# A chunked linear recurrence rewritten: 64-wide corner products, the inverse built apart from its right side, output and norm by token tile

## The chip, the cores and the metric

The kernel runs on one core of a Trainium2 chip. The metric is the device time of one execution in microseconds. Matrix products run on TensorE (PE), with weights loaded beside them (PEld); VectorE is DVE, ScalarE is ACT, GpSimd is POOL; SyncE (SP) issues DMAs. Each engine works through its own queue in order and waits on semaphores that other engines raise.

## What is computed

A model of two layers over 512 tokens of width 1024, and a third block of another kind. Each layer has feed-forward blocks, window attention, a gated memory (mlstm) and the recurrence that is changed here, with 4 heads of 64. For each head, token by token, the reference computes:

```python
def step(state, xs):
    r_t, w_t, k_t, v_t, a_t, b_t = xs
    sa = jnp.einsum('bhvk,bhk->bhv', state, a_t)
    state = (state * w_t[:, :, None, :] + sa[..., None] * b_t[:, :, None, :]
             + v_t[..., None] * k_t[:, :, None, :])
    return state, jnp.einsum('bhvk,bhk->bhv', state, r_t)
```

Ahead of it kk (the key times k_k, made unit length by head) gives a = -kk and b = kk times the rate. Behind it y is centred and normed by head, scaled by ln_w and ln_b, given the bonus sum(r k r_k) v, and multiplied by a gate.

## The kernel before

The stages of a layer run one after another, with a barrier of all engines between them: dense block, window attention, mlstm, `rwkv_stage` (L1340), dense block. In the dense blocks fp32 data are split in two parts and weights stream in by DMA. In `rwkv_stage` all data are in SBUF already, but for four small loads (L1395 to L1398).

Features lie on partitions, tokens on columns: 256 features are two tiles j of 128, with two heads each (halves q). The recurrence is done in chunks of 64 tokens. A token tile t of 128 holds two chunks, so its pair matrices are 128x128 with two blocks of 64x64 on the diagonal that count; masks put zeros elsewhere.

*Opening* (L1411 to L1434, L1564 to L1586, L1621 to L1661). The squares of kk are summed by head with a product by `halves` over 512 columns (L1413). DVE limits them (L1626), ACT takes roots (L1569), DVE takes reciprocals of 128x512 (L1631) and multiplies (L1632), `unit(0)` ahead of the two scans of L1638 and `unit(1)` behind them. Small products give decay, rate and gate (L1418 to L1425). ACT takes exponentials; DVE makes the factors f_a and f_b, POOL makes f_r and f_k (L1405, L1407).

*Tile loop* (L1487). `turn` transposes the factors of a tile to token rows, `pair` makes five pair matrices a head, DVE masks them (L1669), `a_values` (L1479) makes the right side X. Six steps follow. Each squares N and its transpose (L1498, L1502), which ACT (L1601) and DVE (L1687) copy out of PSUM, and adds N's power times X to X (L1507, L1691), X having 128 columns a head. Parts of the next tile's `prepare` stand between the steps. Then come the local products (L1517, L1523, L1524) and each chunk's step of state, G and H (L1531 to L1535).

*State loop* (L1539, L1705), behind all tiles: for 8 chunks PE makes G times state (L1543) and the state's share of y (L1549); DVE makes `carried` (L1709, L1711) and the next state (L1715).

*Norm* (L1552 to L1559, L1720 to L1737), over all 512 tokens with features on partitions: mean and variance with `halves`, root on ACT (L1615), reciprocal of 128x512 (L1732), and three more operations on DVE for each j.

Two pieces of code elsewhere matter for comparison: `mlstm_stage` has products of 128x128 by 65 columns (L1198), and `head_norm_stage` sums squares by token with two-column products (L1800).

## Time and profile before

| | us |
|---|---|
| median of 3 runs | 3401.26 (3397.11 to 3402.22) |
| profiled execution, its own time | 3395.85 |
| its span, first to last instruction | 3394.1 |
| PE busy | 3159.9 (93%) |
| DVE busy | 1449.1 (43%) |
| ACT busy | 1112.5 (33%) |
| mean granted TensorE clock | 0.947 of 2.4 GHz |

The span is the profiled execution between its first and last instruction; 1.75 us of the time lie around it. The clock is granted by a throttle in two levels, 1.2 and 2.4 GHz, and the page gives it as a share: 0.5 and 1.0. `rwkv_stage` runs from 686.3 to 848.1 us in the first layer and from about 2000 to 2165.1 in the second.

### The profile page before, as it was taken

Reading aid. Unit: us, or ns where it says so; the run is one execution under the profiler, and the core shown is the slowest. Engines: PE = TensorE matmul, PEld = TensorE weight load, DVE = VectorE, ACT = ScalarE, POOL = GpSimd, SP = SyncE. Lnnn points to the kernel's source line nnn. Section 1 sums busy time; section 2 is a strip of 40 time slices with the busy share of each in tenths; the row PEclk is TensorE's granted clock in tenths of the full one; section 3 lists DMA queues with packets and bytes.
Section 4 is the critical chain, followed back from the end, with each engine's and each line's share of the span. In section 5 each row is a group of like instructions: output and inputs, shape, how many; then the busy total and the mean of one; then the engine's idle time right before and its main releaser. Section 6 shows DMA issues by size and latency. Waiting matters only on the chain. (4 is left out here: it accounts for less than half of the span.)

```text
span 3394.1 us, 39653 instructions
## 1 busy us (share of the span) xinstructions
PE 3159.9 (93%) x16542; PEld 2654.7 (78%) x16542; DVE 1449.1 (43%) x1897; ACT 1112.5 (33%) x1566; POOL 174.1 (5%) x143
## 2 busy tenths in 40 slices
PE   8999997767999999999999769799999999999999
PEld 7888886556888878888887649588887877888887
DVE  3333414565433336233332564633325327555542
ACT  3222322331422236222222332322225335434431
POOL 0000005400000000000001620000000000000000
PEclk9999998688999999999999759899999989999999
DMA  3323221000223342223402000212234110122332
GB/s 131 100 93 112 94 75 41 1 12 1 100 81 99 110 139 75 75 94 112 136 32 90 1 11 1 94 40 97 99 106 144 50 57 25 44 72 91 97 97 83
DMA packets 71473, 255.64 MB, mean 75 GB/s; under 512 B 8056, under 2 KB 8952, under 8 KB 71296
## 3 DMA queue, kind: packets, MB, share of 16 engines
q1 hardware_dynamic: 71296, 253.12, 22.5%
q8 instruction: 131, 2.15, 0.3%
q14 instruction: 46, 0.38, 0.0%
HBM read 250.99 MB, written 2.10 MB: 75 GB/s over the span
## 5 line engine op out<-in xcount | busy, mean ns | idle before, releaser
L206 PE MATMUL ps<-h_hi,w_space 128*128 128x512 f32 (+3 forms) x5440 | 1504.8, 363 | 17.1 <-DVE h_lo L304 17.1
L206 PEld LDWEIGHTS ps<-h_hi,w_space 128*128 128x128 f32 x5440 | 982.0, 190 | 177.4 <-DVE h_lo L304 20.5
L194 DVE TENSOR_TENSOR w_space<-w_raw,w_space 128x1024 fp32r<-128x1024 f32 x440 | 536.2, 1225 | 1224.2 <-ACT w_space L187 1223.9
L206 PE MATMUL ps<-h_lo,w_space 128*128 128x512 f32 (+3 forms) x2720 | 986.1, 363 | 0.0
L187 ACT CAST w_space<-w_raw 128x1024 fp32r<-128x1024 f32 x440 | 457.9, 1047 | 1124.0 <-PE ps L206 726.0
L216 PE MATMUL ps<-w_space 128*128 128x512 f32 x3312 | 766.2, 393 | 35.0 <-DVE w_space L194 34.1
L216 PEld LDWEIGHTS ps<-w_space 128*128 128x128 f32 x3312 | 625.4, 190 | 166.9 <-issue 31.5
L206 PEld LDWEIGHTS ps<-h_lo,w_space 128*128 128x128 f32 x2720 | 516.5, 190 | 78.6
L579 ACT CAST w_space<-act_p 128x512 fp32r<-128x512 f32 x88 | 54.6, 621 | 187.4 <-DVE act_p L591 172.4
L594 DVE TENSOR_TENSOR w_space<-act_p,w_space 128x512 fp32r<-128x512 f32 x88 | 60.9, 693 | 69.9 <-ACT w_space L579 69.9
L591 DVE TENSOR_TENSOR act_p<-act_s,ps 128x512 f32<-128x512 f32 x88 | 59.9, 681 | 71.3 <-PE ps L206 71.3
L851 POOL MEMSET attn_v_tok<- 128x8 f32 x2 | 0.2, 114 | 1685.9 <-POOLq L86 1685.9
L264 ACT ACTIVATE junk<-x 128x1024 bf16<-128x1024 f32 x40 | 42.3, 1057 | 91.9 <-DVE x L285 80.5
L304 DVE TENSOR_TENSOR h_lo<-ps,h_hi 128x1024 fp32r<-128x1024 f32 x40 | 48.8, 1220 | 52.9 <-ACT h_hi L272 52.9
L216 PE MATMUL ps<-w_space,h_hi 128*128 128x512 f32 x256 | 69.2, 392 | 1.7 <-DVE h_lo L304 1.7
L575 ACT ACTIVATE act_s<-ps 128x512 f32<-128x512 f32 x88 | 52.2, 593 | 56.4 <-PE ps L206 56.4
L246 PE MATMUL ps<-mats,h_tokens 128*128 128x128 f32 x320 | 45.1, 287 | 22.5 <-DVE h_tokens L297 22.5
L628 ACT COPY proj<-ps 128x512 f32<-128x512 f32 x62 | 36.3, 585 | 83.5 <-PE ps L206 83.5
L1687 DVE COPY rwkv_power_t<-ps 128x512 f32<-128x512 f32 x40 | 27.7, 691 | 82.7 <-PE ps L1502 82.7
L2088 ACT ACTIVATE attn_probs<-ps 128x512 f32<-128x512 f32 x64 | 38.3, 599 | 71.3 <-PE ps L1998 71.0
L246 PEld LDWEIGHTS ps<-mats,h_tokens 128*128 128x128 f32 x320 | 38.9, 148 | 28.3 <-issue 13.9
L2008 PEld LDWEIGHTS ps<-v_tok,attn_probs 128*128 128x128 f32 x512 | 59.5, 192 | 1.3
(325 smaller groups left out, 2886.8 us busy)
## 6 DMA issues: line engine op xcount, KB each, us to landing
w_raw<-in_w_ffn_in SPq DMA_DIRECT2D x176, 512.0 KB, 3.5
w_raw<-in_w_ffn_out SPq DMA_DIRECT2D x88, 512.0 KB, 3.5
w_raw<-in_w_in SPq DMA_DIRECT2D x64, 512.0 KB, 3.6
w_raw<-in_w_up SPq DMA_DIRECT2D x44, 512.0 KB, 3.6
w_raw<-in_w_out SPq DMA_DIRECT2D x24, 512.0 KB, 3.6
w_raw<-in_w_down SPq DMA_DIRECT2D x22, 512.0 KB, 3.6
w_raw<-in_w_ple_gate SPq DMA_DIRECT2D x16, 512.0 KB, 5.0
gain_pre<-in_gains_pre SPq DMA_DIRECT2D x10, 512.0 KB, 4.6
```

What stands on the lines that cost most here:

```text
L187: nc.scalar.copy(self.hi(n), self.raw[:, n % SLOTS, :]).then_inc(self.hi_ready, 1)
L194: nc.vector.tensor_tensor(self.lo(n), self.raw[:, n % SLOTS, :], self.hi(n).bitcast(F32), ALU.subtract).then_inc(self.lo_ready, 1)
L206: m = nc.tensor.matmul(c.ps[:, bank, t], part[:, cols], moving[:, k, t], start=(k == 0 and i == 0), stop=(k == KD - 1 and i == 2))
L216: m = nc.tensor.matmul(c.ps[:, bank + half, :], x, part[:, half * S:(half + 1) * S], start=(first and i == 0), stop=(final and i == 2))
L246: m = nc.tensor.transpose(c.ps[:, self.bank(n) + k // 4, (k % 4) * P:(k % 4 + 1) * P], c.hn[:, k * P:(k + 1) * P], c.mat["ident"])
L264: nc.scalar.activation(c.junk[:, :], c.x[:, n, :], ACT.Square, accum_out=c.sums[:, 1, n:n + 1]).then_inc(c.pre_summed, 1)
L304: nc.vector.tensor_tensor(c.h_lo[:, :, t], pair(c, self.bank(n)).rearrange("p (k m) -> p k m", k=KD), c.h_hi[:, :, t].bitcast(F32), ALU.su ...
L575: nc.scalar.activation(c.s[:, q % 2, :], c.ps[:, self.bank(n), :], ACT.Silu).then_inc(c.silu_ready, 1)
L579: nc.scalar.copy(self.a.hi(q), c.p[:, q % 2, :]).then_inc(c.act_hi, 1)
L591: nc.vector.tensor_tensor(c.p[:, q % 2, :], c.s[:, q % 2, :], c.ps[:, self.bank(n), :], ALU.mult).then_inc(c.product, 1)
L594: nc.vector.tensor_tensor(self.a.lo(q), c.p[:, q % 2, :], self.a.hi(q).bitcast(F32), ALU.subtract).then_inc(c.act_ready, 1)
L2008: m = nc.tensor.matmul(c.ps[:, 5 + h % 2, at:at + DH + 1], probs[:, h % 2, j, n * P:(n + 1) * P], c.v_tok[:, j, v, :], start=(j == 0), sto ...
```

## The change

- In the opening the squares are summed by token: 16 products of 128 tokens by 2 columns. Floor, root and reciprocal then work on 128x16. ACT widens the result to 128x512 (`kk_wide`), PE transposes it back, and `unit` multiplies from PSUM; both units stand behind the scans.
- Pair matrices of a, and all that is built from them, are kept as 64x64 corners: chunk k on partition half k. A square is 16 products of 64x64 by 64, in one PSUM bank, copied by ACT alone.
- The inverse T is built by itself in five steps (identity + N, then T + power times T) of 64x64 by 64, and applied once to the right side (`solve`, 128 columns a head).
- State, output and norm of tile t-1 stand inside the loop of tile t. The output is made with tokens on partitions (`outputs`, 16 products of 128x128 by 64). The norm by token is a reduction over 64 columns a head; then two transposes (`turn_back`) and the last operations (`finish`).
- POOL zeroes `r_prime` once. The warm-up root on ACT (L1586) goes. The masks are a third of their size.

The order of PE's queue is in the diff; ACT's and DVE's follow it. DVE's order in tile t is: local and carry of t-1, inverse 1 and 2, next state, carry, inverse 3, next state, masks of a for t+1, centre, inverse 4, masks of r, corner values, variance, inverse 5, norm, finish. The diff is cut by 12 columns on the left; removed lines of the tile loop are those of the listing.

```diff
+    nc.gpsimd.memset(r_prime[:, :, :, :, :], 0.0).then_inc(padded, 1)
...
+    pe.wait_ge(kk_squared, 2)
     for j in range(2):
-        pe.wait_ge(kk_squared, j + 1)
-        nc.tensor.matmul(c.ps[:, 6 + j, :], c.mat["halves"], sq[:, j, :], start=True,
-                         stop=True).then_inc(kk_summed, 1)
+        for n in range(NT):
+            at = (j * NT + n) * 2
+            m = nc.tensor.matmul(c.ps[:, 6, at:at + 2], sq[:, j, n * P:(n + 1) * P],
+                                 c.mats[:, MATS.index("halves"), 0:P:DH], start=True, stop=True)
+    m.then_inc(kk_summed, 1)
...
+    for j in range(2):
+        pe.wait_ge(kk_widened, j + 1)
+        for n in range(NT):
+            m = nc.tensor.transpose(c.ps[:, 6 + j, n * P:(n + 1) * P], kk_wide[:, j, n, :, :], c.mat["ident"])
+        m.then_inc(kk_spread, 1)
     for j in range(2):
         pe.wait_ge(bonus_in, j + 1)
+        pe.wait_ge(lora_out, 4)
...
+    def corners(t, left, right, q, at):
+        for j in range(2):
+            for k in range(2):
+                cols, to = slice(t * P + k * CHUNK, t * P + (k + 1) * CHUNK), (2 * at + j) * CHUNK
+                m = nc.tensor.matmul(c.ps[half(k), ROW_BANKS[q], to:to + CHUNK], left[half(q), j, cols],
+                                     right[half(q), j, cols], start=True, stop=True)
+        return m
+    def pairs_of_a(t):
+        if t:
+            pe.wait_ge(gh_copied, 2 * (t - 1))
+        for q in range(2):
+            corners(t, f_a, f_b, q, N_LOW)
+            corners(t, f_b, f_a, q, N_UP)
+            m = corners(t, f_k, f_a, q, AK)
+        m.then_inc(pairs, 1)
...
+    def pairs_of_r(t):
+        pe.wait_ge(tok_ready, 2 * (t + 1))
         cols = slice(t * P, (t + 1) * P)
+        for o, left in ((RB, f_b), (RK, f_k)):
             for j in range(2):
+                for q in range(2):
+                    to = (2 * o + j) * P
+                    m = nc.tensor.matmul(c.ps[:, (AB_BANK, KV_BANK)[q], to:to + P], left[half(q), j, cols],
+                                         f_r[half(q), j, cols], start=True, stop=True)
+        m.then_inc(pairs, 1)
...
     def a_values(t):
+        pe.wait_ge(masked, 2 * t + 1)
+        for h, j, rows in heads:
+            for k in range(2):
+                m = nc.tensor.matmul(c.ps[half(k), ROW_BANKS[0], h * DH:(h + 1) * DH], pair_t[half(k), t % 2, AK, h, :],
+                                     tok[half(k), t % 3, QV, h * DH:(h + 1) * DH], start=True, stop=True)
         m.then_inc(av_done, 1)
...
+    def square(t, i):
+        n, n_t = parts(t, i - 1)
+        if i == 1:
+            pe.wait_ge(masked, 2 * t + 1)
+            if t:
+                pe.wait_ge(power_ready, STEPS * t)
+        else:
+            pe.wait_ge(power_ready, STEPS * t + i - 1)
+        for o, (a, b) in enumerate(((n_t, n), (n, n_t))):
+            if o == 0 or i < STEPS:
+                for h, j, rows in heads:
+                    for k in range(2):
+                        at = (o * R_HEADS + h) * CHUNK
+                        m = nc.tensor.matmul(c.ps[half(k), SQ_BANK, at:at + CHUNK], a[half(k), h, :],
+                                             b[half(k), h, :], start=True, stop=True)
+        m.then_inc(squared, 1)
+    def inverse(t, i):
+        pe.wait_ge(power_ready, STEPS * t + i)
+        if i == 1:
+            pe.wait_ge(t_first, t + 1)
+            if t:
+                pe.wait_ge(x_copied, t)
+        else:
+            pe.wait_ge(t_ready, STEPS * t + i - 1)
+        for h, j, rows in heads:
+            for k in range(2):
+                m = nc.tensor.matmul(c.ps[half(k), T_BANK, h * CHUNK:(h + 1) * CHUNK], parts(t, i)[0][half(k), h, :],
+                                     T[half(k), t % 2, h, :], start=True, stop=True)
+        m.then_inc(t_done, 1)
+    def solve(t):
+        pe.wait_ge(t_ready, STEPS * (t + 1))
+        pe.wait_ge(av_copied, t + 1)
+        for h, j, rows in heads:
+            for k in range(2):
+                m = nc.tensor.matmul(c.ps[half(k), T_BANK, h * P:(h + 1) * P], T[half(k), t % 2, h, :],
+                                     tok[half(k), t % 3, QA:QX + 1, h * DH:(h + 1) * DH], start=True, stop=True)
+        m.then_inc(x_done, 1)
+    def local(t):
+        pe.wait_ge(x_copied, t + 1)
+        pe.wait_ge(masked, 2 * (t + 1))
+        if t:
+            pe.wait_ge(state_ready, 2 * t + 1)
+        for h, j, rows in heads:
+            m = nc.tensor.matmul(c.ps[rows, S_BANK, j * P:(j + 1) * P], X[:, t % 2, h, 0, :], r_t[:, t % 2, RB, h, :],
+                                 start=True, stop=True)
+        m.then_inc(r_done, 1)
+    def steps_of_state(t):
+        pe.wait_ge(av_copied, min(t + 2, NT))
+        for k in range(2):
+            for h, j, rows in heads:
+                hc, at = slice(h * DH, (h + 1) * DH), j * P
+                nc.tensor.matmul(c.ps[rows, ROW_BANKS[k], at:at + DH], X[half(k), t % 2, h, 0, :],
+                                 tok[half(k), t % 3, QB, hc], start=True, stop=True)
+                o = c.ps[rows, ROW_BANKS[k], at + DH:at + P]
+                nc.tensor.matmul(o, tok[half(k), t % 3, QB, hc], X[half(k), t % 2, h, 1, :], start=True, stop=False)
+                m = nc.tensor.matmul(o, tok[half(k), t % 3, QK, hc], tok[half(k), t % 3, QV, hc], start=False,
+                                     stop=True)
+            m.then_inc(gh_done, 1)
+    def next_state(n):
+        t = n // 2
+        pe.wait_ge(gh_copied, n + 1)
+        pe.wait_ge(r_ready, t + 1)
+        pe.wait_ge(state_ready, n + 1)
+        for h, j, rows in heads:
+            at = 2 * P + j * DH
+            m = nc.tensor.matmul(c.ps[rows, S_BANK, at:at + DH], GH[rows, t % 2, n % 2, j, 0:DH],
+                                 state[rows, n, j, :], start=True, stop=True)
+        m.then_inc(state_done, 1)
+    def outputs(t):
+        pe.wait_ge(r_ready, t + 1)
+        pe.wait_ge(state_ready, 2 * t + 2)
+        if t:
+            pe.wait_ge(out_ready, t)
+        for h, j, rows in heads:
+            o = c.ps[:, Y_BANK, h * DH:(h + 1) * DH]
+            nc.tensor.matmul(o, r_t[:, t % 2, RB, h, :], X[:, t % 2, h, 1, :], start=True, stop=False)
+            nc.tensor.matmul(o, r_t[:, t % 2, RK, h, :], tok[:, t % 3, QV, h * DH:(h + 1) * DH], start=False, stop=False)
+            for k in range(2):
+                m = nc.tensor.matmul(o, r_prime[:, j, h % 2, k, :], state[:, 2 * t + k, j, :], start=False, stop=(k == 1))
+        m.then_inc(y_done, 1)
+    def turn_back(t):
+        pe.wait_ge(normed, t + 1)
+        for j in range(2):
+            m = nc.tensor.transpose(c.ps[:, Y_BANK, (2 + j) * P:(3 + j) * P], y[:, 2 * j:2 * j + 2, :],
+                                    c.mat["ident"])
+        m.then_inc(turned_back, 1)
...
     for t in range(NT):
+        more = t + 1 < NT
+        square(t, 1)
+        if t:
+            local(t - 1)
+            steps_of_state(t - 1)
+        square(t, 2)
+        inverse(t, 1)
+        if more:
+            turn(t + 1)
+        square(t, 3)
+        inverse(t, 2)
+        if t:
+            next_state(2 * t - 2)
+        square(t, 4)
+        inverse(t, 3)
+        if t:
+            outputs(t - 1)
+            next_state(2 * t - 1)
+        if more:
+            pairs_of_a(t + 1)
+        square(t, 5)
+        inverse(t, 4)
+        if more:
+            pairs_of_r(t + 1)
+        inverse(t, 5)
+        if more:
             a_values(t + 1)
+        if t:
+            turn_back(t - 1)
+        solve(t)
+    local(NT - 1)
+    steps_of_state(NT - 1)
+    next_state(NCH - 2)
+    outputs(NT - 1)
+    turn_back(NT - 1)
...
-        act.wait_ge(kk_floor, j + 1)
-        nc.scalar.activation(kk_len[:, j, :], kk_len[:, j, :], ACT.Sqrt).then_inc(kk_root, 1)
+    act.wait_ge(kk_floor, 1)
+    nc.scalar.activation(kk_len[:, :, :, :], kk_len[:, :, :, :], ACT.Sqrt).then_inc(kk_root, 1)
     nc.scalar.activation(lora[:, 1, :], mix[:, G_T, :], ACT.Sigmoid).then_inc(lora_in, 1)
     for j in range(2):
-        act.wait_ge(lora_done, j + 1)
...
+        powers(t, 1)
+        if t:
+            steps_of_state(t - 1)
+        powers(t, 2)
+        if t + 1 < NT:
+            rows_of(t + 1)
+        for i in range(3, STEPS + 1):
+            powers(t, i)
+        if t:
+            squares(t - 1)
+            root(t - 1)
+        solution(t)
+    steps_of_state(NT - 1)
+    squares(NT - 1)
+    root(NT - 1)
...
-    for j in range(2):
-        dve.wait_ge(kk_summed, j + 1)
-        nc.vector.tensor_scalar(kk_len[:, j, :], c.ps[:, 6 + j, :], 1e-24, None, ALU.max).then_inc(kk_floor, 1)
+    dve.wait_ge(kk_summed, 1)
+    nc.vector.tensor_scalar(kk_len[:, :, :, :].rearrange("p j n q -> p (j n q)"), c.ps[:, 6, 0:4 * NT], 1e-24,
+                            None, ALU.max).then_inc(kk_floor, 1)
+    dve.wait_ge(kk_root, 1)
+    nc.vector.reciprocal(kk_len[:, :, :, :], kk_len[:, :, :, :]).then_inc(kk_inverted, 1)
 
     def unit(j):
-        dve.wait_ge(kk_root, j + 1)
+        dve.wait_ge(kk_spread, j + 1)
         dve.wait_ge(kk_raw, 2)
-        ch.link(nc.vector.reciprocal(kk_len[:, j, :], kk_len[:, j, :]))
-        ch.link(nc.vector.tensor_tensor(kk[:, j, :], kk[:, j, :], kk_len[:, j, :], ALU.mult))
...
+    def centre(t):
+        dve.wait_ge(y_done, t + 1)
+        if t:
+            dve.wait_ge(turned_back, t)
+        o = by_head(quarter(Y_BANK, 0))
+        nc.vector.tensor_reduce(y_mean[:, :], o, AX, ALU.add).then_inc(y_summed, 1)
+        dve.wait_ge(y_summed, t + 1)
+        nc.vector.scalar_tensor_tensor(out=y[:, :, :], in0=y_mean[:, :].unsqueeze(2).to_broadcast([P, R_HEADS, DH]),
+                                       scalar=-1.0 / DH, in1=o, op0=ALU.mult, op1=ALU.add).then_inc(centred, 1)
+    def variance(t):
+        dve.wait_ge(y_squared, t + 1)
+        nc.vector.tensor_reduce(y_var[:, :], y_sq[:, :, :], AX, ALU.add).then_inc(var_summed, 1)
+    def norm(t):
+        dve.wait_ge(var_root, t + 1)
+        nc.vector.reciprocal(y_inv[:, :], y_var[:, :]).then_inc(var_inverted, 1)
+        dve.wait_ge(var_inverted, t + 1)
+        nc.vector.tensor_tensor(y[:, :, :], y[:, :, :], y_inv[:, :].unsqueeze(2).to_broadcast([P, R_HEADS, DH]),
+                                ALU.mult).then_inc(normed, 1)
+    def finish(t):
+        cols = slice(t * P, (t + 1) * P)
+        dve.wait_ge(turned_back, t + 1)
+        for j in range(2):
+            ch.link(nc.vector.tensor_scalar(out[:, j, :], c.ps[:, Y_BANK, (2 + j) * P:(3 + j) * P], vcol("ln_w", j),
+                                            vcol("ln_b", j), ALU.mult, ALU.add))
+        ch.link(nc.vector.tensor_tensor(out[:, :, :], out[:, :, :], bonus[:, :, cols], ALU.add))
+        nc.vector.tensor_tensor(c.y[:, 6:8, cols], out[:, :, :], gate[:, :, cols], ALU.mult).then_inc(out_ready, 1)
+    ch.wait()
+    dve.sem_inc(state_ready, 1)
+    dve.wait_ge(padded, 1)
```

## Rows read from the trace of the kernel before

**Rows 1.** Busy time by stretch of core 0, with granted clock (PEclk).

```profile
core 0: us, PE busy (x) PEld busy (x) DVE busy (x) ACT busy (x) POOL busy (x), PEclk, DMA share, GB/s
640.00:682.00 42.00, 35.16 (x108) 24.43 (x107) 25.46 (x67) 9.62 (x21) 15.94 (x16) 0.50 0.00 1
686.30:715.60 29.30, 11.68 (x20) 3.56 (x20) 24.57 (x26) 16.89 (x24) 6.36 (x4) 0.67 0.10 32
715.60:724.65 9.05, 6.56 (x56) 5.76 (x56) 5.02 (x13) 1.48 (x3) 0.00 (x0) 0.81 0.01 2
748.88:773.10 24.22, 23.34 (x259) 22.08 (x257) 11.75 (x23) 5.43 (x11) 0.00 (x0) 1.00 0.01 1
818.80:821.50 2.70, 1.36 (x32) 1.12 (x32) 2.34 (x10) 0.00 (x0) 0.00 (x0) 1.00 0.03 6
821.50:830.00 8.50, 6.72 (x96) 5.59 (x96) 7.13 (x31) 0.00 (x0) 0.00 (x0) 0.50 0.00 0
830.00:848.10 18.10, 6.19 (x8) 1.97 (x8) 13.76 (x12) 2.56 (x4) 0.00 (x0) 0.69 0.00 0
2029.10:2165.10 136.00, 112.80 (x1160) 101.19 (x1160) 71.47 (x146) 24.45 (x48) 0.00 (x0) 0.88 0.00 1
```

**Rows 2.** Timeline of PE, tile from 748.88: start, us, line, shapes, count.

```profile
747.17 0.32 PE L1531 MATMUL ps<-rwkv_tok,rwkv_x 64*64 64x64 f32 x2
...
749.87 1.06 PE L1502 MATMUL ps<-rwkv_n_t,rwkv_n 128*128 128x128 f32 x8
...
755.30 1.26 PE L1457 MATMUL ps<-proj 64*128 64x128 f32 x16
...
769.88 0.66 PE L1517 MATMUL ps<-rwkv_rb_t,rwkv_x 128*64 128x128 f32 x8
```

**Rows 3.** Timeline of PE and DVE in the state loop.

```profile
818.93 0.45 PE L1543 MATMUL ps<-rwkv_state,rwkv_gh 64*64 64x64 f32 x8 [0.64 <-DVEq L1704]
...
819.65 0.47 DVE L1715 SCALAR_TENSOR_TENSOR rwkv_state<-ps,rwkv_decay,rwkv_carried 128x64 f32<-128x64 f32 x2
...
821.64 0.69 PE L1543 MATMUL ps<-rwkv_state,rwkv_gh 64*64 64x64 f32 x8 [0.72 <-DVEq L1719]
```

**Rows 4.** Durations of single records by line: ns min/median/max.

```profile
L1543 PE MATMUL ps<-rwkv_state,rwkv_gh x128: 218/311/366, 818.9 to 2145.6; 64*64 64x64 f32 x128
...
L1444 PE MATMUL ps<-mats,proj x64: 272/273/447, 715.7 to 2093.2; 128*128 128x128 f32 x64
...
L1198 PE MATMUL ps<-mlstm_v_tok,mlstm_weighted x160: 417/417/477, 645.9 to 1993.1; 128*128 128x65 f32 x160
```

**Rows 5.** Timeline of PE at the lower clock.

```profile
675.12 4.53 PE L1198 MATMUL ps<-mlstm_v_tok,mlstm_weighted 128*128 128x65 f32 x20 [1.81 <-DVE mlstm_weighted L1311]
...
715.66 1.94 PE L1444 MATMUL ps<-mats,proj 128*128 128x128 f32 x8 [2.21 <-DVE proj L1657]
```

**Rows 6.** Timeline of ACT, DVE and POOL in the opening.

```profile
687.85 1.15 ACT L1565 ACTIVATE rwkv_sq<-rwkv_kk 128x512 f32<-128x512 f32 x2 [5.68 <-DVE rwkv_kk L1622]
...
700.15 0.69 DVE L1641 TENSOR_TENSOR proj<-rwkv_cum,rwkv_sig_w 128x512 f32<-128x512 f32 x1
...
706.95 1.65 POOL L1407 TENSOR_TENSOR proj<-rwkv_sig_w,rwkv_grow 128x512 f32<-128x512 f32 x1 [4.97 <-DVE rwkv_sq L1650]
...
707.50 1.37 DVE L1646 TENSOR_SCALAR rwkv_sig_w<-rwkv_rate,vecs 128x512 f32<-128x512 f32 x1
```

**Rows 7.** The head norm's sum by token: timeline, and durations by line.

```profile
2775.84 1.84 PE L1800 MATMUL ps<-mats,headnorm_sq 128*128 128x2 f32 x8 [0.44 <-ACT headnorm_sq L1846]
...
L1800 PE MATMUL ps<-mats,headnorm_sq x104: 167/251/354, 2767.6 to 2794.8; 128*128 128x2 f32 x104
```

**Rows 8.** Timeline of DVE in the norm.

```profile
836.74 3.35 DVE L1732 RECIPROCAL rwkv_cum<-rwkv_cum 128x512 f32<-128x512 f32 x1 [1.41 <-ACT rwkv_cum L1615]
```

**Rows 9.** Timeline of ACT and DVE in the tile from 748.88.

```profile
753.62 0.59 ACT L1601 COPY rwkv_power<-ps 128x512 f32<-128x512 f32 x1 [2.97 <-PE ps L1498]
...
769.98 0.42 DVE L1675 COPY rwkv_x<-ps 128x256 f32<-128x256 f32 x1
```

416 lines of the change are left out of this document (186 added, 230 removed).

## The prediction

> **What bounds the kernel now.** I read the page first: PE is busy 93% of the span and the chain that ended last is dense products, so a stage is worth what its own last wait is worth. The change touches only the recurrence, which runs once in each of two layers, so I cut the trace there. The table by stretch [rows 1] shows the first run: an opening on DVE and ACT of 29.3 us, 9.05 us of first pairs, three token tiles of 24.2 us from 724.65 on and a last one that is left with 21.5, a state loop of 11.2 (818.80 to 830.00) and a norm of 18.1. From the first transpose (715.66) to the last DVE instruction (848.08) that is 132.4 us; the second run takes 136.0 (2029.16 to 2165.1). Barriers stand at both ends, so what the stage loses or gains the kernel does.
>
> In a tile PE is busy 23.3 of 24.2 us: it is the bound there. In the state loop and the norm it is not; there DVE and PE hand one small thing back and forth [rows 3], and the norm has two reciprocals of 3.35 us [rows 8].
>
> The last thing to see is the clock. It stands at 1.00 (2.4 GHz) through the tiles, whose products are 128x128, and in 818.80 to 821.50. Then, with nothing in the queue but 64x64 products, it is at 0.50 (1.2 GHz), although PE is busy 6.7 of 8.5 us. The stretch 640 to 682 of the stage before has PE busy 84% and the clock at 0.50 throughout [rows 1]. So on this kernel a busy queue does not by itself hold the upper level.
>
> **PE's price for each shape.** A merged row less its last product, over the products before it, gives the step (two records make one fp32 product, one a transpose). At the upper level: 128x128 on 128 columns, (1.06 - 0.27)/7 = 0.112 us a record, the transposes of L1444 alike; 64 rows with 128 columns, (1.26 - 0.27)/15 = 0.066; 128x128 on 64 columns is taken like the full one, 0.11 (its weights are as wide); 128x64 on 128 columns, (0.66 - 0.27)/7 = 0.055; the 48 records of 64x64 from 747.17 to the next tile at 748.88, 0.036 [rows 2]; 64x64 on the two diagonal quarters in turn, (0.45 - 0.22)/7 = 0.033 [rows 3, 4]. At the lower: the same quarters (0.69 - 0.31)/7 = 0.054 [rows 3]; a transpose (1.94 - 0.45)/7 = 0.213; 128x128 on 65 columns (4.53 - 0.42)/19 = 0.216 [rows 5]. The shapes with no row at the lower level lie between their upper price and twice it; since 0.112 becomes 0.213 and 0.11 becomes 0.216, I take near twice: 0.107 where two tiles overlap, 0.057 for the 0.036. The new product of the solution, 64x64 on 128 columns, has no row: at least 0.033, at most 0.112; I take 0.055, its nearest, and 0.107.
>
> **The loop over tiles.** A tile in the middle, by records. Quarters: squares 4x32 + 16, inverse 5x16, corner values 16, two states 16, together 256 (once 128 of the full ones). Pairs of a and the state's steps: 96 at the 0.036 price. Transposes forth and back: 10. Outputs by token, four products a head with 128-column weights: 32. Pairs of r: 16. Local 8 and solution 16: 24.
> - Upper: 256x0.033 + 96x0.036 + 10x0.112 + 32x0.11 + 16x0.066 + 24x0.055 = 8.4 + 3.5 + 1.1 + 3.5 + 1.1 + 1.3 = 18.9 us.
> - Lower: 13.8 + 5.5 + 2.1 + 6.9 + 1.7 + 2.6 = 32.6 us.
>
> To these come handovers. Tile 748.88 sums by the same prices to 128x0.112 + 40x0.066 + 8x0.112 + 8x0.11 + 24x0.055 + 48x0.036 = 21.8 of its 24.2 us, so 2.4 us of switching and waiting. After, one wait is plain: the back transpose asks for the norm, and variance stands on DVE behind the corner copy, then root on ACT, reciprocal and product on DVE (0.42 + 0.42 + 0.3 + 0.2 + 0.42 with hops of 0.04 to 0.14), and the solution stands behind it on PE: 2.2 us. With 1.2 for switches that is 3.4 at the lower level (36.0 us a tile) and, with a wait for the last inverse step, 4.2 at the upper (23.1). DVE has about 12 us and ACT about 6 in a tile (a copy of 512 columns on ACT 0.59, one of 256 on DVE 0.42 [rows 9]): neither is the bound. That squares are copied by ACT alone costs 0.1 in copy, and is hidden while PE works on the inverse.
>
> The first tile lacks state, outputs and back transpose: 240x0.054 + 48x0.057 + 8x0.213 + 16x0.107x2 = 20.8 and 3.2 of waits = 24.0 (upper 15.9). The last lacks transposes, pairs and corner values (7.0): 29.0 (18.4). The opening pairs: 7.2 (4.8).
>
> **The end.** State loop and norm over 512 columns go (29.3 us). In their place stands, after the last solution: copy and local 2.0, state's steps 2.7, the carry and next state 2.4 (0.47 on DVE for the state itself [rows 3], as much for the carry, the rest hops), outputs 7.0, centre, square, variance, root, reciprocal, product 3.3, back transpose and four last operations 2.0: about 18.7 with 0.7 less of outputs and steps hidden; at the upper level 13.2.
>
> Lower level: 7.2 + 24.0 + 36.0 + 36.0 + 29.0 + 18.7 = 150.9, against 132.4 and 136.0: +18.5 and +14.9. Upper: 4.8 + 15.9 + 23.1 + 23.1 + 18.4 + 13.2 = 98.5: -33.9 and -37.5.
>
> **The opening on DVE.** Two reciprocals of 512 columns (6.7 us) leave DVE's path. In comes a sum by token: 16 products of two columns with 128-column weights, 32 records. The head norm's row gives (1.84 - 0.25)/7 = 0.23 us a record [rows 7]; at the transposes' 0.213, which lies next to it, they take 6.8 us, from the end of ACT's squares at 689.0 [rows 6] to 696.0. Square root, a table load, ACT's sigmoid and two copies of 0.6 follow, and the lora products stand behind the 32 records on PE, so ACT gives the first decay input at 700.1 and both scans and differences end at 703.9; before, the last of them, L1641, ended at 700.8 [rows 6]. The reciprocal that stood behind it is gone, but a second unit product (0.69) and POOL's first operation come in: a DVE instruction waits out POOL's (L1646 took 1.37 beside POOL's 1.65 [rows 6], twice what its plain form takes). I get +0.7 us a layer; bounds -2.5 (records at 0.112) to +2.5 (all four POOL operations in the way). POOL's memset of r_prime is unpriced, between 0.2 and 3.3 (two POOL operations), and has 25 us before anyone asks. The mask load shrinks behind other loads: nothing. A square-root table load moves to the second tile, 1.3 at most, beside DVE's variance.
>
> **Which level.** Full-array products give way to quarters with waits between them; the only such stretch in the trace lost the upper level. I take the lower, with one short upper stretch a layer (transposes and pairs raised it at 715.60 [rows 1]), worth 1.5 each. Sum: 18.5 + 14.9 + 1.4 - 3.0 = +32 us on the profiled 3395.85; that run is 5.4 under the median of those shown, 3401.26. The prediction is 3433.
>
> The Trainium skill, "TensorE: Matmul & The Clock Gate", Part 1, says the lower level is the default and that activity lifts it; by that rule read as busy time, this loop, busy nine tenths, would keep 2.4 GHz and the sum would be the upper one. The row of 640 to 682, 84% busy at 0.50, speaks against reading it so.
>
> **Rivals.**
> - *The loop keeps the upper level, but for a few falls* (PE leaves the bound mostly; this ends on the other side). For it: PE never idles over 2.2 us in a tile, and 64-row pairs in the opening ran with the clock up. Against: 821.50 to 830.00. It decides once the granted clock of the middle tiles reads above 0.9. -33.9 - 37.5 + 1.4 = -70 if it never falls, with cold openings and a fall in each tile -60: 3341. The point where it turns: a middle tile under about 30 us.
> - *Half and half*: outputs, transposes and pairs of r lift the level once a tile and quarters drop it. Between the sums, middle tiles of 29 to 30 us: +8, 3409.
> - *The change doesn't shorten the end*, because outputs by token (32 records a tile at 0.216) only trade the norm for PE time: that is inside the first sum; without the end's saving of 10.6 us a layer the time would be 3454. For it speaks only the wait for the norm.
>
> **Chances.** Lower level 0.51, half and half 0.16, upper 0.30, long end 0.03. Within 0.2% (about 7 us) of 3401 is what a measurement here can't tell from no change. Of the half case 0.06 lies below, 0.04 within, 0.06 above; of the lower case 0.02 below. Faster 0.38, same 0.04, slower 0.58. The likeliest case alone reaches from 3415 to 3446 (PE steps 6% off, opening bounds). The range takes in the upper case: 3332 to 3446.
>
> **What would show it.** The clock in the tile loop: 0.5 to 0.6 bears me out, 0.9 the rival. L1543's successors and the squares at 0.054 a record. A middle tile of 36 us against 23. The end at 19 us after the last solution. The opening at 30 us, with the sum by token at 6.8. Wrong would be: quarters that hold the clock at 1.00, or steps of quarters under 0.05 at the lower level.

## The result, and the profile after

The changed kernel takes 3317.73 us (median of 4 runs, 3314.60 to 3323.63) against 3400.45 us before (4 runs, 3397.11 to 3402.22). The ratio is 0.976, with a 95% interval of 0.9743 to 0.9777: 83 us faster. The forecast was 3433, with a range down to 3332; the result lies outside it on the fast side, past even the rival at 3341. The profiled execution took 3315.65 us, its span is 3313.8, and its mean granted clock 0.950.

Granted clock and busy time by stretch, changed kernel, first run of the stage (opening, first pairs, four tiles, end), then three stretches of 3.4 us (two around the end of the second tile, one in the last tile), then opening and rest of the second run:

```profile
core 0: us, PE busy (x) PEld busy (x) DVE busy (x) ACT busy (x) POOL busy (x), PEclk, DMA share, GB/s
685.90:711.60 25.70, 14.55 (x40) 7.59 (x40) 16.84 (x23) 15.38 (x23) 6.92 (x5) 0.63 0.09 26
711.60:718.80 7.20, 7.16 (x88) 6.51 (x90) 3.50 (x7) 1.07 (x2) 0.00 (x0) 0.50 0.01 2
718.80:733.70 14.90, 13.07 (x336) 12.17 (x334) 5.84 (x13) 3.79 (x7) 0.00 (x0) 0.93 0.01 3
733.70:755.50 21.80, 19.19 (x440) 17.92 (x437) 11.10 (x33) 7.12 (x13) 0.00 (x0) 0.99 0.01 2
755.50:778.40 22.90, 20.29 (x438) 18.82 (x436) 11.62 (x34) 5.83 (x12) 0.00 (x0) 0.94 0.01 3
778.40:796.00 17.60, 15.36 (x350) 14.08 (x344) 9.02 (x30) 4.83 (x11) 0.00 (x0) 1.00 0.01 3
796.00:809.20 13.20, 7.04 (x98) 6.22 (x98) 6.53 (x20) 1.98 (x5) 0.00 (x0) 0.89 0.01 1
751.60:755.00 3.40, 1.55 (x32) 1.25 (x29) 2.63 (x8) 0.95 (x2) 0.00 (x0) 1.00 0.00 0
755.00:758.40 3.40, 3.40 (x49) 2.95 (x45) 1.15 (x3) 1.17 (x2) 0.00 (x0) 0.51 0.02 5
792.00:795.40 3.40, 1.65 (x29) 1.38 (x31) 2.35 (x8) 0.71 (x2) 0.00 (x0) 1.00 0.00 0
1961.60:1987.20 25.60, 14.10 (x41) 7.34 (x41) 16.81 (x24) 15.38 (x23) 6.91 (x5) 0.63 0.09 26
1987.20:2083.60 96.40, 80.71 (x1728) 74.49 (x1728) 47.51 (x133) 24.63 (x49) 0.00 (x0) 0.92 0.01 2
```

These answer to [rows 1]. The tiles hold 0.93 to 1.00. The level comes up at 720.9, 2 us into the first tile; from there on no stretch of the tiles is at 0.50 but 3.4 us from 755.0, behind a stretch in which PE was busy 1.55 of 3.4 us. In the second run it is again one stretch of 3.4 us (2028.2). Against the stretches of before: opening 28.3 to 25.7 us in both layers; first transpose to last DVE operation 132.4 to 97.5 and 136.0 to 96.3. Together that is 5.3 + 34.9 + 39.7 = 79.9 of the 80.3 us by which the span got shorter. The rest of the kernel together moved by 0.4 us.

PE in the changed kernel, by timeline:

```profile
718.82 1.92 PE L1512 MATMUL ps<-rwkv_pair_t 64*64 64x64 f32 x32
721.43 1.15 PE L1512 MATMUL ps<-rwkv_power 64*64 64x64 f32 x32 [0.69 <-ACT rwkv_power L1676]
...
732.75 1.09 PE L1536 MATMUL ps<-rwkv_tok,rwkv_inverse_t 64*64 64x128 f32 x16 [0.92 <-DVE rwkv_inverse_t L1807]
...
753.97 0.44 PE L1590 MATMUL ps<-mats,rwkv_y 128*128 128x128 f32 x2 [1.84 <-DVE rwkv_y L1864]
...
806.67 0.69 PE L1590 MATMUL ps<-mats,rwkv_y 128*128 128x128 f32 x2 [2.88 <-DVE rwkv_y L1864]
```

A square of 32 records takes 1.92 us at 0.50 and 1.15 at 1.00: (1.92 - 0.31)/31 = 0.052 and (1.15 - 0.22)/31 = 0.030 a record, where the sum had 0.054 and 0.033 [rows 3, 4]. The solution, (1.09 - 0.27)/15 = 0.055 a record, is as assumed.

The opening, ACT and DVE beside PE, which answers to [rows 6] and [rows 7]:

```profile
687.61 3.57 PE L1417 MATMUL ps<-mats,rwkv_sq 128*128 128x2 f32 x16 [3.84 <-ACT rwkv_sq L1641]
...
691.68 0.25 DVE L1728 RECIPROCAL rwkv_kk_len<-rwkv_kk_len 128x16 f32<-128x16 f32 x1 [0.28 <-ACT rwkv_kk_len L1644]
...
694.97 1.27 ACT L1651 ACTIVATE rwkv_sig_w<-ps,vecs 128x512 f32<-128x512 f32 x2 [0.36 <-PE ps L1426]
695.76 1.23 DVE L1738 TENSOR_TENSOR_SCAN rwkv_cum<-rwkv_reset,rwkv_sig_w 128x512 f32<-128x512 f32 x1 [3.83 <-ACT rwkv_sig_w L1651]
```

The sum by token is 16 records, where the prediction had 32. The code issues eight products for it (two tiles of features times four of tokens), not 16 as was said of the change; at two records a product, as everywhere, that is 16.

### The profile page after: what moved, and what is told of

The parts are those of the page before. It is cut to its first block and busy times, and to the rows that moved or that the text cites. A ratio compares the mean times of both kernels' runs of the same rounds, so it can differ in the third digit from the quotient of the medians.

```text
span 3313.8 us, 42013 instructions
## 1 busy us (share of the span) xinstructions
PE 3106.2 (94%) x17718; PEld 2614.0 (79%) x17718; DVE 1385.5 (42%) x1867; ACT 1109.9 (33%) x1566; POOL 175.5 (5%) x145
## 5 line engine op out<-in xcount | busy, mean ns | idle before, releaser
L206 PEld LDWEIGHTS ps<-h_hi,w_space 128*128 128x128 f32 x5440 | 981.7, 190 | 177.8 <-DVE h_lo L304 20.3
L216 PE MATMUL ps<-w_space 128*128 128x512 f32 x3312 | 767.9, 393 | 15.9 <-DVE w_space L194 15.0
L2266 ACT ACTIVATE attn_probs<-ps 128x512 f32<-128x512 f32 x64 | 38.3, 599 | 71.4 <-PE ps L2176 71.1
L272 ACT CAST h_hi<-ps 128x1024 fp32r<-128x1024 f32 x40 | 40.3, 1007 | 57.6 <-PE ps L246 57.6
```

The lines of the kernel that those rows point to most:

```text
L206: m = nc.tensor.matmul(c.ps[:, bank, t], part[:, cols], moving[:, k, t], start=(k == 0 and i == 0), stop=(k == KD - 1 and i == 2))
L216: m = nc.tensor.matmul(c.ps[:, bank + half, :], x, part[:, half * S:(half + 1) * S], start=(first and i == 0), stop=(final and i == 2))
```

## The experiments

Two questions: what holds or drops the clock in this stage, and what each part of the change is worth. "Theory A" is one and the same in all of them: PE's waits between products let the clock fall, whatever the products' shape. "Fillers" are products or transposes whose result nobody reads, put where PE would wait. The same kernel's median moves by some us between chips, so each run's ratio is to runs of the kernel before on its own chip (0.976 for the changed kernel), and profiles are compared by the length of the stage, first to last DVE operation: 160.7 and 164.3 us before, 123.3 and 122.0 after. Medians that differ by 3 to 7 us can have overlapping intervals; where they do, the text says so.

| run | median us | ratio (95%) | stage, layer 1 / 2 |
|---|---|---|---|
| state_filled (of before) | 3397.43 | 0.9997 (0.9986 to 1.0009) | 163.1 / 163.2 |
| new_opening (of before) | 3392.77 | 0.9981 (0.9970 to 0.9993) | 157.6 / 158.2 |
| copy_six | 3397.26 | 0.9998 (0.9983 to 1.0012) | 166.5 / 160.3 |
| squares_twice | 3354.47 | 0.9866 (0.9851 to 0.9880) | 140.7 / 138.9 |
| norm_behind | 3335.62 | 0.9810 (0.9787 to 0.9832) | 129.8 / 127.4 |
| state_behind | 3364.52 | 0.9895 (0.9872 to 0.9918) | 150.8 / 145.4 |
| behind_filled | 3352.59 | 0.9850 (0.9821 to 0.9879) | 137.4 / 137.1 |
| back_late | 3320.85 | 0.9765 (0.9751 to 0.9780) | 123.5 / 123.1 |
| back_mid | 3324.13 | 0.9780 (0.9761 to 0.9798) | 125.7 / 126.2 |
| opening_filled | 3316.56 | 0.9751 (0.9731 to 0.9771) | 119.5 / 120.4 |
| end_filled | 3319.66 | 0.9766 (0.9747 to 0.9786) | 125.5 / 122.0 |
| all_filled | 3308.07 | 0.9728 (0.9707 to 0.9749) | 117.5 / 117.3 |
| lora_first | 3306.71 | 0.9730 (0.9708 to 0.9752) | 116.8 / 118.0 |
| outputs_split | 3301.45 | 0.9707 (0.9686 to 0.9729) | 115.0 / 116.3 |

### Fillers in the old state loop (state_filled)

```diff
                         m.then_inc(y_state, 1)
+                    for i in range(8):
+                        rows = slice(DH * (i % 2), DH * (i % 2) + DH)
+                        nc.tensor.matmul(c.ps[rows, 5, 0:DH], c.mat["ident"][rows, 0:DH], c.mat["halves"][rows, 0:DH],
+                                         start=True, stop=True)
```

> The kernel before, with eight products of 64x64 on the two quarters (16 records) added behind each of the eight steps of the state loop, into a bank that nobody reads, where PE waits 0.64 to 0.72 us for DVE in each step. Theory A (waits between the products let the clock fall, whatever their shape): the granted clock stays at 1.00 through the state loop, where it read 0.50 from 821.5 to 830.0, and the loop of 11.2 us gets 1 to 1.5 us shorter a layer, 3396 to 3400 in all. Theory B (as the prediction took it: a queue of nothing but 64x64 products doesn't hold the upper level): 0.50 as before, the fillers take 16 x 0.054 = 0.9 us a step at that level and overhang the wait by 0.2, so the loop gets 1 to 2 us longer a layer, 3403 or more.

Its state loop ran from 823.5 to 834.7. By stretch:

```profile
814.70:818.10 3.40, 1.68 (x15) 1.33 (x14) 1.81 (x3) 0.00 (x0) 0.00 (x0) 1.00 0.00 0
818.00:821.50 3.50, 3.42 (x33) 3.09 (x35) 0.45 (x2) 0.37 (x1) 0.00 (x0) 0.51 0.00 0
821.50:834.70 13.20, 10.62 (x301) 9.41 (x297) 9.47 (x40) 0.75 (x2) 0.00 (x0) 1.00 0.01 2
```

On DVE, the seventh of eight equal steps and the start of the eighth:

```profile
831.92 0.29 DVE L1713 TENSOR_TENSOR rwkv_carried<-rwkv_state,rwkv_gh 128x128 f32<-128x128 f32 x1
832.24 0.42 DVE L1715 TENSOR_SCALAR rwkv_carried<-rwkv_carried,rwkv_decay 128x64 f32<-128x64 f32 x2
832.70 0.47 DVE L1719 SCALAR_TENSOR_TENSOR rwkv_state<-ps,rwkv_decay,rwkv_carried 128x64 f32<-128x64 f32 x2
833.32 0.29 DVE L1713 TENSOR_TENSOR rwkv_carried<-rwkv_state,rwkv_gh 128x128 f32<-128x128 f32 x1
```

The loop holds nothing but 64x64 products, and the clock read 1.00 throughout, where it fell to 0.50 before. That bears out theory A on the clock: the waits drop it, the shape doesn't. Its time was wrong: the loop still takes 11.2 us, a step 1.40, because DVE's chain (carried, carried, state) sets the step at either level. Here, where PE isn't the bound, the level that came back gave nothing. The stages are 2.4 us longer and 1.1 shorter than before's; outside the loop the clock fell at other places (818.1 here, 821.5 there), and the median is the same. The first two rows are worth a look too: in the second, PE is busy 3.42 of 3.50 us with the clock at 0.51, and in the 3.4 us ahead of it PE had been busy only 1.68. The level of a stretch answers to what PE did before it.

### Waits put into the new tiles (copy_six)

```diff
                     else:
+                        for dst in (cum[:, 0, :], cum[:, 1, :], rate[:, 0, :], rate[:, 1, :], sig_w[:, 0, :]):
+                            nc.scalar.copy(dst, c.ps[:, SQ_BANK, :])
                         nc.scalar.copy(power[:, i % 2].rearrange("p o h n -> p (o h n)"), c.ps[:, SQ_BANK, :]).then_inc(power_ready, 1)
```

> The changed kernel, with ACT copying each of the first four squares six times (five extra copies of 0.59 us into tiles that are free by then). PE's instructions are unchanged; only waits come in. A square is 1.1 us of PE, then 3.5 of ACT, so a middle tile would be some 5 x 4.9 + 5 = 28 to 30 us if PE kept the upper level, with PE busy about 19 of them. Theory A (waits let the clock fall): the granted clock reads 0.50 in a good part of the tiles, the middle tile is over 31 us, the kernel 3375 or more. Theory B' (the mix of shapes sets the level, and this mix holds it): the clock stays at 1.00 but for what it falls now, the middle tile is 27 to 29, the kernel 3345 to 3370.

Its two middle tiles of the first layer, which run the same instructions, and PE's waits in the second of them:

```profile
744.90:772.80 27.90, 20.36 (x440) 18.72 (x438) 11.69 (x34) 16.62 (x33) 0.00 (x0) 0.95 0.01 2
772.80:806.50 33.70, 26.80 (x436) 25.04 (x434) 11.74 (x35) 15.34 (x32) 0.00 (x0) 0.75 0.01 2
```

```profile
777.36 1.15 PE L1512 MATMUL ps<-rwkv_power 64*64 64x64 f32 x32 [0.85 <-ACT rwkv_power L1678]
...
781.64 1.15 PE L1512 MATMUL ps<-rwkv_power 64*64 64x64 f32 x32 [1.64 <-ACT rwkv_power L1678]
...
785.92 1.15 PE L1512 MATMUL ps<-rwkv_power 64*64 64x64 f32 x32 [2.43 <-ACT rwkv_power L1678]
```

With waits of 0.85, 1.64 and 2.43 us ahead of the squares the clock falls again and again (mean of the span 0.934 against 0.950), and the change's whole gain is gone. Not all of these 80 us are the clock's: the waits by themselves were put at 3345 to 3370, and 3397.26 lies 27 to 52 us above that. Theory A holds. Its bound of 31 us for a middle tile is passed by three of four: 33.7 in the first layer, 33.4 and 33.8 in the second. It is the step that the prediction got wrong seen from the other side: this mix of shapes loses the upper level when it is made to wait. It doesn't lose it at every such wait. The tile of 27.9 us runs the same instructions with nearly the same waits (0.84, 1.64, 2.43) at 0.95; the record doesn't show what spared it.

### Double squares (squares_twice)

```diff
-                    for o, (a, b) in enumerate(((n_t, n), (n, n_t))):
+                    for o, (a, b) in 2 * tuple(enumerate(((n_t, n), (n, n_t)))):
```

> The changed kernel, with every product of a square issued twice (144 records more a tile, same result). If PE is the bound in the tiles at the upper level, each record costs the step of a quarter product, 0.033: 144 x 0.033 = 4.8 us a tile, 19 a layer, +38 in all (3356), and the clock stays up. If ACT, DVE or the chain of handovers is the bound, part of it is hidden: under +20. If many quarter products lower the level, the tiles go to twice their length: over +100.

The tile from 737.25 takes 26.2 us instead of 21.8: 4.4 us for 144 records, 0.031 each. The time rose by 37, where +38 was expected of a PE-bound tile. PE is the bound in the new tiles too, and a quarter record costs what its step says.

### The opening alone (new_opening)

The kernel before with the changed kernel's lines for `kk_len`, `kk_wide`, the products for w and a, and `unit` (one place of many shown):

```diff
-                    ch.link(nc.vector.reciprocal(kk_len[:, j, :], kk_len[:, j, :]))
-                    ch.link(nc.vector.tensor_tensor(kk[:, j, :], kk[:, j, :], kk_len[:, j, :], ALU.mult))
+                    dve.wait_ge(kk_spread, j + 1)
+                    ch.link(nc.vector.tensor_tensor(kk[:, j, :], kk[:, j, :], c.ps[:, 6 + j, :], ALU.mult))
```

> The kernel before with the changed kernel's opening alone (lengths of kk by a sum by token of 16 two-column products, square root, reciprocal of 16 columns, widened and transposed back, both unit products behind the scans). In the two traces the stretch from the first DVE operation of the stage to the first transpose went from 28.3 to 25.8 us in the one layer and from 28.4 to 25.9 in the other. Theory (the opening gains by itself, the 16 records at 0.215 taking 3.6 us where two reciprocals took 6.7): -2.5 us a layer, -5 in all, 3391. Rival (the prediction's +0.7 a layer was right, and the 2.5 come of what stands behind the opening): 3397 or more.

5.8 us faster in the median, with an interval from 2.4 to 10; the first transposes come 25.4 and 25.7 us after the stage's start (685.56 in the first layer), where it was 28.3:

```profile
710.92 1.94 PE L1453 MATMUL ps<-mats,proj 128*128 128x128 f32 x8 [2.05 <-DVE proj L1668]
```

The opening gains by itself (its sum by token is eight products here too, where the expectation says 16); the 0.7 us a layer that the prediction added to it aren't there. The stage of the second layer is 6.1 us shorter, more than the opening gives: it also lacks a fall of the clock that the profile of the kernel before has around the start of the first tile (0.50 from 2036.6 to 2043.5).

### Work put back behind the tiles (norm_behind, state_behind, behind_filled)

norm_behind keeps `centre` in the tile and moves the rest of the norm:

```diff
-                    if t:
-                        norm(t - 1)
-                        finish(t - 1)
...
+                for t in range(NT):
+                    variance(t)
+                for t in range(NT):
+                    norm(t)
+                    if t:
+                        finish(t - 1)
+                finish(NT - 1)
```

> The changed kernel, with each tile's centring kept where it is and its variance, root, norm, back transpose and last operations done for all four tiles behind the last one (y of four tiles kept). Out of the tiles go the wait for the norm (1.84 us in two middle tiles, 1.1 in the last), 0.44 of PE and 3 us of DVE: 6 to 8 us a layer with the fall of the clock. Onto the end come three more variances at about 1 us each, three norms of 0.7 and three finishes of 2.3: 10 to 14 us. Theory (the norm by token tile pays because it hides): +4 to +14 in all, 3322 to 3332. Rival (the wait it puts into the tiles costs what it hides): within 4 us of the changed kernel or under it.

+18 us, where +4 to +14 was expected: the tiles got shorter (20.2 and 20.3 us), the end longer.

```profile
793.00:817.10 24.10, 8.96 (x104) 7.03 (x104) 13.67 (x39) 4.55 (x11) 0.00 (x0) 0.66 0.00 1
```

The theory's sign holds, its size was short. The clock stood at 0.66 over the end, but PE was busy only 8.96 of 24.1 us there; how much of the miss is the clock was not tried.

state_behind moves the states and outputs as well:

```diff
+                for t in range(NT):
+                    next_state(2 * t)
+                    outputs(t)
+                    if t + 1 < NT:
+                        next_state(2 * t + 1)
+                    if t:
+                        turn_back(t - 1)
```

> The changed kernel, with the next states, the outputs by token and the whole norm of all four tiles done behind the last tile, in a pipeline over tiles (r and its masks, values, solutions and the state's factors kept for four tiles; local parts and the state's steps stay in the tiles). Out of each of the tiles 1 to 3 go 3.6 us of outputs, 0.8 of states, 0.44 of back transpose and up to 1.84 of waiting for the norm on PE: a middle tile should take 16 to 17 us instead of 21.8 to 22.9, -16 to -18 a layer. Behind come three tiles of the pipeline, bound by DVE (two carries and states 2.4, centring 0.84, variance 0.42, norm 0.6, last operations 1.7, hops) at 6.5 to 8 us: +20 to +24, and the clock may fall there. Theory (overlap gains only what PE and DVE can share, because the tiles are bound by PE: most of the 41 us a layer are shorter work, not hiding): +4 to +8 us a layer, 3325 to 3335. Rival (the change's gain is mainly that the end is hidden in the tiles): +15 a layer or more, over 3348.

The theory fell, the rival's number holds: 3364.5, +47. A middle tile takes 15.4 us, but the pipeline behind takes 14.1 a tile, where 6.5 to 8 was expected. By stretch, and on PE:

```profile
736.22:751.64 15.42, 14.28 (x388) 13.32 (x386) 6.14 (x15) 5.12 (x10) 0.00 (x0) 1.00 0.01 3
784.50:839.40 54.90, 33.64 (x182) 30.87 (x180) 20.14 (x65) 4.14 (x9) 0.00 (x0) 0.50 0.00 1
```

```profile
810.73 0.66 PE L1595 MATMUL ps<-proj,rwkv_kk_wide 128*128 128x64 f32 x2 [4.96 <-DVE rwkv_state L1842]
```

I had taken DVE's and PE's parts as overlapping. They take turns: PE waits 4.96 us for DVE's norm and state, then DVE waits 7.05 us for the outputs, which cost 7.0 at 0.50. To separate the clock from the turns, the same kernel with fillers in those waits:

```diff
                     next_state(2 * t)
+                    fill(40 if t else 7)
                     outputs(t)
```

> The run with state, outputs and norm behind the tiles (3364.5; granted clock 0.50 for 61 us from the last tile on, 14.1 us for each tile of the pipeline behind, of which 7.0 are outputs at that level and some 7 DVE's chain), with transposes of constants on PE while it waits there for DVE (40 a tile, fewer at the first and the last). Theory A (part of what overlap gives is the clock: alone behind the tiles the outputs run at the lower level): the clock stays at 1.00, outputs take 3.6 us, a tile of the pipeline 10.5, the stage 13 to 16 us a layer shorter, 3333 to 3340, so that some 20 of the 47 us are work hidden and the rest the clock. Rival (all 47 are handovers that the overlap hides): within 6 us of 3364.

```profile
776.60:823.50 46.90, 40.47 (x423) 37.43 (x419) 22.90 (x75) 5.47 (x12) 0.00 (x0) 1.00 0.00 1
```

The clock stays at 1.00, a tile of the pipeline takes 10.4 us, and the stage is 13.4 and 8.3 us shorter. The median, 3352.59, lies between the two forecasts (3333 to 3340, and within 6 of 3364). The median falls by 12 of the 47 us, the profiled times by 19.4 of 60.2 (3375.86 to 3356.42, with 3315.65 for the changed kernel; the first of these is 11 us over its own median). So a quarter to a third of what the overlap is worth is the clock, and the rest is work hidden, as far as the fillers themselves cost nothing, which was not tried; I had expected more than half to be the clock.

### The wait for the norm taken away (back_late, back_mid)

back_late moves the back transpose and the last operations of all three tiles into the next tile; back_mid those of the first two:

```diff
                     square(t, 1)
+                    if t > 1:
+                        turn_back(t - 2)
...
-                    if t:
+                    if t and not more:
                         turn_back(t - 1)
                     solve(t)
```

> The changed kernel, with the back transpose of a tile and its four last DVE operations moved from before the solution of the next tile to behind the first square (PE) and the carry (DVE) of the tile after that. In the changed kernel PE waits 1.84 us for the norm there in each of three tiles, and the granted clock falls for 3.4 us right behind one such wait in each layer (755.0, 2028.2). Theory A: the wait goes, 1.5 to 2 us a tile, and the falls with it, 1.5 to 2 us each: 3.5 to 8 us a layer, 7 to 15 in all (3303 to 3311). Rival: DVE has the same operations in the way of the inverse instead (1.7 us of last operations ahead of an inverse step), so PE waits there: within 3 us of the changed kernel.

> The changed kernel, with the back transpose and last operations moved behind the next tile's first square and carry for the first two tiles only; the third's stay in the last tile, ahead of its solution, as in the changed kernel. In the run with all three moved the middle tiles took 20.55 and 20.91 us instead of 21.8 and 22.9, and the last tile with the end 34.4 instead of 30.8. Theory (the gain in the middle was given back on DVE's path of the end): the middle tiles as there, the last tile and the end as in the changed kernel, -3.3 us a layer, -6.6 in all: 3311. Rival (the clock falls somewhere else instead): within 3 us of the changed kernel.

Neither gained. The medians are 3 and 6 us over the changed kernel's, with intervals that overlap its own; in the profiles back_mid's stages are 2.4 and 4.2 us longer. Its tiles did what was expected, 20.54 and 20.90 us at 1.00. Then:

```profile
790.60:794.00 3.40, 1.78 (x32) 1.50 (x34) 2.35 (x8) 0.71 (x2) 0.00 (x0) 1.00 0.00 0
794.00:812.90 18.90, 12.81 (x106) 11.33 (x102) 6.96 (x21) 2.04 (x5) 0.00 (x0) 0.50 0.00 1
812.90:821.30 8.40, 4.83 (x12) 3.80 (x12) 6.89 (x8) 7.67 (x11) 0.00 (x0) 0.50 0.70 238
```

The level fell behind the waits of the last tile (0.85 and 1.06 us), the end stayed at 0.50 with its own waits, and the next dense stage began there too. The changed kernel has the same two waits at the same places, PE busy 1.65 of 3.40 us from 792.0, and came through at 1.00. So these waits can drop the level and need not; which of the two happens, no run here shows a rule for. The rival "the clock falls somewhere else instead" holds.

### Fillers in the new kernel (opening_filled, end_filled, all_filled)

```diff
                     m.then_inc(kk_spread, 1)
+                pe.wait_ge(lora_out, 4)
+                fill(24)
                 for j in range(2):
+                    if j:
+                        fill(24)
                     pe.wait_ge(bonus_in, j + 1)
...
+                fill(16)
```

where `fill` issues transposes of constants into a bank that nobody reads.

> The changed kernel, with 24, 24 and 16 transposes of constants that nobody reads put on PE where it waits in the opening (behind the transposes of kk, behind the first and behind the second bonus sum). Theory A (waits lower the clock, and it stays up if PE has work): the granted clock stays at 1.00 from 697 to the tiles, where it read 0.50 from 703.8 to 720.9; first pairs 4.8 to 5.2 us instead of 7.2, the first square 1.1 instead of 1.9: 2.5 to 3.3 us a layer, 5 to 6.6 in all (3311 to 3313). Rival: the fillers at 0.213 each (13.6 us) delay the bonus sum and the first turn by up to 3 us: 3317 to 3324.

> The changed kernel, with 5 to 24 transposes of constants on PE at each of its waits in the last tile and behind it (71 in all). The outputs of the last tile ran at 1.00 already in the changed kernel's profile; the clock fell at 806.2 for 10.2 us. Theory A: no fall before the stage's end, gain under 1 us a layer in the stage, and the next stage's first products may start at 1.00: 3312 to 3317. Rival: fillers sized at 0.112 each that overhang the waits: 3318 to 3323.

> The changed kernel with the first two tiles' back transposes moved as before (back_mid: middle tiles 20.5 and 20.9 us, but the clock at 0.50 from 794.0 for 27.3 us, and no gain), the fillers of the opening and those of the last tile and the end. Theory A (what took the gain of the moved transposes was the clock at the end, which falls where PE waits): the clock stays at 1.00 from 697 to the end of the stage, last tile and end 30 to 31 us, -3.3 a layer for the middle tiles and -2.5 for the opening: 3304 to 3308. Rival (the end was longer for another reason, DVE's path): the clock stays up and the end takes 33 us or more all the same: 3311 or more.

opening_filled, its opening in two parts and its first pairs:

```profile
687.20:703.00 15.80, 13.65 (x60) 9.31 (x60) 7.19 (x12) 14.17 (x21) 2.23 (x2) 0.65 0.14 41
703.00:717.20 14.20, 10.62 (x132) 8.71 (x134) 12.59 (x18) 2.29 (x5) 4.72 (x3) 1.00 0.01 1
```

The level stays at 1.00 into the tiles, the pairs take 4.2 us instead of 7.2, and the stages are 3.7 and 1.6 us shorter; in the median (3316.56, where 3311 to 3313 was expected) that is inside the noise. end_filled alone gave nothing, and its 3319.66 lies in the rival's range: the clock did what theory A said (1.00 from 779.7 past the stage's end), but PE had its level at the end already, one more fall came inside the tiles of layer 1, and the fillers overhang the waits. From the last tile's local product to DVE's first operation on the output it is 8.3 us there (795.94 to 804.23) and 7.25 in the changed kernel (796.58 to 803.83). all_filled puts both sets of fillers on back_mid:

```profile
733.20:753.70 20.50, 18.56 (x436) 17.46 (x434) 10.12 (x30) 7.12 (x13) 0.00 (x0) 1.00 0.01 2
753.70:774.70 21.00, 19.06 (x440) 17.79 (x438) 11.70 (x34) 5.84 (x12) 0.00 (x0) 1.00 0.01 4
774.70:793.40 18.70, 18.15 (x370) 16.22 (x367) 10.39 (x32) 5.35 (x11) 0.00 (x0) 1.00 0.01 3
793.40:806.70 13.30, 12.94 (x152) 11.82 (x152) 5.89 (x18) 1.46 (x4) 0.00 (x0) 1.00 0.01 1
```

The moved transposes that gained nothing now give their 3 us a layer, and the end takes 13.3 us again. 16 us separate the medians of back_mid and all_filled (13 in the profiles), and all_filled only adds work to PE; some 5 of them are the opening's, by the stages of opening_filled. Theory A, as expected.

### Two chains shortened (lora_first, outputs_split)

lora_first is all_filled with the products for w ahead of those for a on PE, and on ACT:

```diff
-                for j in range(2):
-                    act.wait_ge(kk_inverted, 1)
-                    nc.scalar.copy(kk_wide[:, j, :, :, :], kk_len[:, j, :, :].unsqueeze(3).to_broadcast([P, NT, 2, DH])).then_inc(kk_widened, 1)
                 for j in range(2):
                     act.wait_ge(lora_done, j + 1)
                     nc.scalar.activation(sig_w[:, j, :], c.ps[:, j, :], ACT.Sigmoid, bias=vcol("w0", j)).then_inc(lora_out, 1)
+                for j in range(2):
+                    act.wait_ge(kk_inverted, 1)
+                    nc.scalar.copy(kk_wide[:, j, :, :, :], kk_len[:, j, :, :].unsqueeze(3).to_broadcast([P, NT, 2, DH])).then_inc(kk_widened, 1)
```

> As the run before it, and in the opening PE does the products for w ahead of those for a, and ACT their sigmoids ahead of the widening. In the changed kernel the first scan waits for the sigmoid of w at 695.76, which waits for PE (694.83) behind the products for a. Theory (the opening is one chain through the scan): the first scan 1.3 to 1.6 us earlier, and the first transpose with it: 3 us under the run before it. Rival (the unit products then wait for the widened lengths, or ACT's six exponentials bind): within 1 us of it.

```profile
693.48 1.23 DVE L1759 TENSOR_TENSOR_SCAN rwkv_cum<-rwkv_reset,rwkv_sig_w 128x512 f32<-128x512 f32 x1 [2.34 <-ACT rwkv_sig_w L1669]
...
697.88 0.69 DVE L1754 TENSOR_TENSOR rwkv_kk<-rwkv_kk,ps 128x512 f32<-128x512 f32 x1 [0.58 <-PE ps L1439]
```

The scan starts 8.4 us after the stage's start instead of 9.9, but the unit product behind it now waits 0.58 for PE: 0.7 and 0.9 us a layer are left up to the first square, too little to measure in the median. The rival holds.

outputs_split splits the last tile's outputs and takes out the fillers of 4, 3 and 7 transposes that stood around there:

```diff
-                fill(4, AB_BANK)
                 steps_of_state(NT - 1)
-                fill(3, AB_BANK)
+                pe.wait_ge(out_ready, NT - 1)
+                free_outputs(NT - 1, range(0, 2))
                 next_state(NCH - 2)
-                fill(7, AB_BANK)
-                outputs(NT - 1)
+                free_outputs(NT - 1, range(2, 4))
+                state_outputs(NT - 1)
```

> The run with all fillers and the products for w first (3306.7), with the last tile's outputs split: the two products a head that need no state go around the next state, where PE waited for the copies and DVE, and only the two with the state (1.8 us) stand behind it. Theory (the end is one chain: state, outputs 3.6, centring to last operations 5.5): the end 1.5 to 1.8 us shorter a layer, 3 to 3.6 in all, 3303. Rival (the free products delay the next state by as much): within 1 us a layer of that run.

The stages are 1.8 and 1.7 us shorter and the median is 5 lower, 3301.45, with an interval that overlaps lora_first's. It (0.9686 to 0.9729) lies wholly under that of the changed kernel (0.9743 to 0.9777): this version beats it. Most of the 1.7 us aren't the split's, though. The last tile's local product and DVE's first operation on the output, in the changed kernel, lora_first and outputs_split:

```profile
796.58 0.66 PE L1546 MATMUL ps<-rwkv_r_t,rwkv_x 128*64 128x128 f32 x8 [0.69 <-ACT rwkv_x L1682]
803.83 0.42 DVE L1851 TENSOR_REDUCE rwkv_y_mean<-ps 128x4 f32<-128x256 f32 x1 [3.90 <-PE ps L1584]
...
788.51 0.66 PE L1554 MATMUL ps<-rwkv_r_t,rwkv_x 128*64 128x128 f32 x8
796.81 0.42 DVE L1872 TENSOR_REDUCE rwkv_y_mean<-ps 128x4 f32<-128x256 f32 x1 [3.89 <-PE ps L1592]
...
786.82 0.66 PE L1554 MATMUL ps<-rwkv_r_t,rwkv_x 128*64 128x128 f32 x8
793.45 0.42 DVE L1887 TENSOR_REDUCE rwkv_y_mean<-ps 128x4 f32<-128x256 f32 x1 [2.27 <-PE ps L1594]
```

That is 7.25, 8.30 and 6.63 us, all at 1.00. By the kernel without fillers 1.05 us of the 1.67 are the fillers' overhang, and 0.6 the split; a run with the split alone was not made. The four heads share one PSUM bank, so only the first product of all clears it. The Trainium skill, "PSUM — Partial Sum Buffer", The four PSUM rules, says that the first product of a group clears the written marks of the whole bank, on the partitions that it writes; no run here shows what a second clearing would do.

## Why the prediction was wrong

**Which level: the step that failed.** "Full-array products give way to quarters with waits between them; the only such stretch in the trace lost the upper level. I take the lower". That stretch, the old state loop, differs from its neighbours in two things, small products and waits. The step took the new tiles to share its fate, though in them waits are few. With the waits filled, the same quarter products held 1.00 (state_filled); with waits added, the new tiles lost it (copy_six). In the changed kernel's tile from 733.7 PE is idle 2.6 us of 21.8, the longest wait being 1.84, and once the level is up in the tiles it falls for 3.4 us at most. The prediction's own sign of being wrong, quarters that hold the clock at 1.00, came. By the two sums this one step is worth 105 us (33.4 + 71.4). The stretch from 640 to 682 [rows 1], 84% busy at 0.50, that I set against reading the level as activity, has such waits too, up to 1.81 us [rows 5]. That they keep it down was not tried; but its products have weights of 128x128, so it was no evidence on product size.

By that row the prediction also set aside the rule on activity that it had cited. The Trainium skill, "TensorE: Matmul & The Clock Gate", Part 1, A second HAM failure mode, tells of a bf16 kernel in which short idles between groups of products make the clock go up and down. The traces here, of fp32 products, agree: copy_six at 0.75 with waits of 0.85 to 2.43 us, and back_mid at 0.50 behind 0.85 and 1.06.

**PE's prices: right.** Quarters 0.030 and 0.052 where 0.033 and 0.054 were taken, the solution 0.055. The upper sum gave 4.8 + 15.9 + 23.1 + 23.1 + 18.4 + 13.2 = 98.5; measured were 97.5 and 96.3. By its terms, in the first layer: pairs 7.2 (the lower term exactly), tiles 14.9, 21.8, 22.9, 17.6, end 13.2. The wait for the norm was put at 2.2 us and is 1.84.

**The end: right.** 13.2 us from the copy of the last solution on, as in the upper sum, at 1.00 for the first 10 of them.

**The opening: a term mis-sized, sign and all.** +0.7 a layer was forecast, -2.6 and -2.7 came. The sum by token was taken as 16 products, 32 records at 0.213, 6.8 us; it is eight products, 16 records at (3.57 - 0.35)/15 = 0.215, 3.57 us. The price was right and the count twice too high, by the code: its loops are 2 x 4, and [rows 7] has the same form, eight records for the four products of a call. The 3.2 us are nearly the whole difference of 3.3. The bound of -2.5 was missed by 0.1 and 0.2.

**The rivals.** The upper level, given 0.30, is what happened: -71.4 by its sum, -74.6 measured from the first transpose on; with the opening's 5.3 that is the result. The long end did not come. The range ended at 3332, which is this rival without any fall (3401 - 70), and the result lies 14 us under it: 6.7 are the opening's error in both layers, 3.2 are tiles and end a little shorter than summed, and 3.3 come of adding 5.4 us from the profiled execution to the median, which is 2.1 for the changed kernel. So even with the level right the low end of the range was too high, by these three together.

## What to carry to other kernels

Where a stretch of one kernel lost the clock, list everything in which it differs before naming the cause; here PE's waits, of 0.6 to 2.4 us each, did it and product size did not. Judge a change in a PE-bound loop by the waits it leaves, and don't expect a removed wait to pay by itself when others decide the level: back_mid gained nothing, and the same edit with fillers did. Fillers give nothing where another engine sets the step (state_filled), and they cost what they overhang the wait: 1.0 us a layer at the end (end_filled, lora_first). When an edit takes fillers out along with what it tries, count them apart.

## What the runs showed of the hardware

- The granted clock can be 0.51 with PE busy 3.42 of 3.50 us (state_filled) and 1.00 with PE busy 1.55 of 3.40 us (changed kernel, 751.6 to 755.0): the level follows what lay before, in state_filled a stretch with PE busy 1.68 of 3.40 us.
- Tiles of the same instructions took 27.9 and 33.7 us (copy_six), and the same last tile and end 30.8 us in the changed kernel and 36.5 in back_mid, as the level fell or didn't. The same waits don't always drop it.
- A record of a two-column product with 128-column weights takes 0.215 us at the lower level, as much as one of 65 columns (0.216, [rows 5]) and as a transpose of 128 (0.213).
